# A DeltaNet stage on one core: GpSimd's operations in thirds, its substitution behind VectorE's, transposes and projections in another order

## The reference

```
qkv, z, ab = split(h @ w_in)
q, k, v = silu(centred_conv(qkv))                 # width 4, per channel
q = l2norm(q) * 128**-0.5 ; k = l2norm(k)
g, beta from ab                                   # per token, head and direction
# per chunk of C tokens, gc = cumsum(g):
decay = exp(where(i >= j, gc_i - gc_j, -inf))
a_mat = where(i > j, beta_i * (k @ k.T) * decay, 0) + eye(C)
u, w  = solve(a_mat, [v * beta, k * beta * exp(gc)])      # unit lower triangular
qk = (q @ k.T) * decay ; qg = q * exp(gc) ; kd = k * exp(gc_last - gc)
# scan over the chunks:
v_new = u - w @ S ; o = qg @ S + qk @ v_new ; S = S * exp(gc_last) + kd.T @ v_new
o = rmsnorm(o_f + reverse(o_b)) * silu(z) ; out = o @ w_out
```

## Time and profile before

| what | us |
|---|---|
| median of 3 runs | 3733.95 (3731.53 to 3744.8) |
| the profiled execution's own time | 3739.49 |
| its span, first to last instruction | 3737.7 |
| TensorE busy, of the span | 3344.0 (89%) |
| VectorE, GpSimd, ScalarE busy | 2001.9, 1144.6, 1044.5 |

### The profile page before, as it was taken

One profiled execution on the slowest core, in us unless ns is written; L12 is line 12 of the kernel. 1 busy time (PEld: TensorE's weight loads), 2 busy tenths in 40 slices (PEclk: granted clock), 3 DMA queues, 4 the chain that ended last, 5 costly groups with the idle time before them and its releaser, 6 DMA issues. The chain is left out here.

```text
span 3737.7 us, 51893 instructions
## 1 busy us (share of the span) xinstructions
PE 3344.0 (89%) x20310; PEld 3185.9 (85%) x20310; DVE 2001.9 (54%) x2743; ACT 1044.5 (28%) x1619; POOL 1144.6 (31%) x797
## 2 busy tenths in 40 slices
PE   4985699899999999779999989989898999999996
PEld 2982489799999999678888878878787999999995
DVE  8757653653444335856776776776746222232217
ACT  3226440311111111243534534434423111111110
POOL 2213101321212112245654654654533121121211
PEclk7997799999999999889999999999999999999998
DMA  4520101121211121131231231231320111111111
GB/s 166 185 101 8 59 1 43 71 79 63 90 63 68 63 85 63 68 84 39 67 67 40 66 80 26 67 80 26 99 86 29 46 41 46 41 46 40 41 46 68
DMA packets 103577, 237.92 MB, mean 64 GB/s; under 512 B 8108, under 2 KB 61132, under 8 KB 100428
## 3 DMA queue, kind: packets, MB, share of 16 engines
q1 hardware_dynamic: 103372, 234.82, 20.0%
HBM read 217.54 MB, written 17.26 MB: 63 GB/s over the span
## 5 line engine op out<-in xcount | busy, mean ns | idle before, releaser
L55 PE MATMUL psum<-h_high,panel_high 128*128 128x384 f32 x3624 | 1249.7, 345 | 99.8 <-DVE h_low L495 76.7
L56 PE MATMUL psum<-h_low,panel_high 128*128 128x384 f32 x3624 | 1226.5, 338 | 0.0
L57 PE MATMUL psum<-h_high,panel_low 128*128 128x384 f32 x3624 | 1225.8, 338 | 0.0
L187 POOL TENSOR_TENSOR panel_low<-panel_raw,panel_high 128x1024 fp32r<-128x1024 f32 x196 | 486.3, 2481 | 1715.2 <-ACT panel_high L182 1670.4
L55 PEld LDWEIGHTS psum<-h_high,panel_high 128*128 128x128 f32 x3624 | 691.7, 191 | 145.6 <-issue 94.1
L56 PEld LDWEIGHTS psum<-h_low,panel_high 128*128 128x128 f32 x3624 | 693.0, 191 | 0.0
L57 PEld LDWEIGHTS psum<-h_high,panel_low 128*128 128x128 f32 x3624 | 691.7, 191 | 0.0
L847 DVE TENSOR_TENSOR ffn_product<-ffn_silu_gate,psum 128x1152 f32<-128x1152 f32 x44 | 59.6, 1354 | 709.9 <-PE psum L57 708.5
L182 ACT ACTIVATE panel_high<-panel_raw 128x1024 fp32r<-128x1024 f32 x195 | 205.1, 1052 | 628.5 <-PE psum L57 561.1
L55 PE MATMUL psum<-ffn_mid_high,panel_high 128*128 128x384 f32 x1056 | 355.3, 336 | 12.2 <-DVE x L650 7.5
L57 PE MATMUL psum<-ffn_mid_high,panel_low 128*128 128x384 f32 x1056 | 354.3, 335 | 0.0
(11 more groups left out here) (336 smaller groups left out, 4812.1 us busy)
## 6 DMA issues: line engine op xcount, KB each, us to landing
panel_raw<-in_stream SPq DMA_DIRECT2D x197, 512.0 KB, 3.3
ffn_mod_panels<-in_wmod SPq DMA_DIRECT2D x24, 1024.0 KB, 7.6
dn_rep<-blocks_spill SPq DMA_DIRECT2D x16, 1152.0 KB, 7.8
in_mod_panels<-in_wmod SPq DMA_DIRECT2D x16, 1024.0 KB, 5.5
dn_qg<-rows_spill SPq DMA_DIRECT2D x16, 576.0 KB, 15.9
first_mod_panels<-in_wmod SPq DMA_DIRECT2D x8, 1024.0 KB, 14.0
x<-in_x SPq DMA_DIRECT2D x3, 1536.0 KB, 14.3
x<-in_x SPq DMA_DIRECT2D x1, 4608.0 KB, 15.5
```

Of the source, the lines that this page charges most:

```text
L55: pe.matmul(out, wh, xh, start=first, stop=False)
L56: pe.matmul(out, wh, xl, start=False, stop=False)
L57: return pe.matmul(out, wl, xh, start=False, stop=last)
L187: pool.tensor_tensor(self.wl[buf][:], self.raw[buf][:], self.wh[buf][:].bitcast(F32), ALU.subtract).then_inc(self.split_low.sem, 1)
```

## The change

- GpSimd: the whole-width operations (subtracting sums and adding masks in `exponents`, the diagonal masks, both `decayed_q`, both `kd`, `gated`) are issued as three of 384 columns, and `split` in the heads as two halves of 512. The semaphore rises with the last piece.
- GpSimd begins `substitute` for direction 1 only when VectorE has ended direction 0 (`sub_step[0]` at 31 in the head).
- VectorE: the second `expand` stands behind the sixth slot (`EXPAND = 5`), and the fifth step of v's convolution behind the fifth slot instead of the sixth.
- The first step of k's convolution for the next head goes from VectorE to ScalarE, behind its copy of k's last tile.
- TensorE: the transposes of k (`nine(1, dn.kn, None, True)`) come right behind the reading of k by k, ahead of `tile(3, 0)`; the spread for the output's norm behind `tile(3, 0)`; the sums for q behind `tile(3, 1)`. ScalarE takes `k_tok` accordingly earlier.
- The two final products of the scan's first step go to banks 0 and 1 instead of 3 and 4, and the wait for ScalarE's copies of them moves from the scan's first step to the projection group that next writes bank 0.
- SP fetches the next head's first rows when q by k is done, and the second ones when the values are done, as both before.

```diff
@@ SP
                     sp.wait_ge(qg_ready, 2 * h + 2)
+                    sp.wait_ge(grp_full, full_count(h, FULL_QK, True))
+                    rows(h + 1, 0, dn.rows[0]).then_inc(rows_full, 16)
                     sp.wait_ge(u_full, 2 * h + 2)
-                    for d in range(2):
-                        rows(h + 1, d, dn.rows[d]).then_inc(rows_full, 16)
+                    rows(h + 1, 1, dn.rows[1]).then_inc(rows_full, 16)
@@ GpSimd
             def split(h, j):
-                s.pool_split(pool, 4 * h + (p0 + j), (p0 + j) % 2)
+                p, buf = 4 * h + (p0 + j), (p0 + j) % 2
+                pool.wait_ge(s.split_high.sem, p + 1)
+                for half in (slice(0, 512), slice(512, 1024)):
+                    i = pool.tensor_tensor(s.wl[buf][:, half], s.raw[buf][:, half], s.wh[buf][:, half].bitcast(F32),
+                                           ALU.subtract)
+                i.then_inc(s.split_low.sem, 1)
+
+            def thirds(op):
+
+                for n in range(0, NT, 3):
+                    i = op(slice(n, n + 3))
+                return i
...
-                    mul(dn.osum[:], dn.osum[:], dn.silu_z[:]).then_inc(y_done, 1)
+                    o, z = by_block(dn.osum), by_block(dn.silu_z)
+                    thirds(lambda n: mul(o[:, n], o[:, n], z[:, n])).then_inc(y_done, 1)
...
                 if not first:
                     gated(h)
+                pool.wait_ge(sub_step[0], 31 * h + 31)
                 substitute(pool, 1, h)
@@ TensorE
                     if m == (24 if k_reads == 1 else 40):
                         pe.wait_ge(k_read, k_reads)
+                    if m == 24 and k_reads > 1:
+                        pe.wait_ge(fin_ready, 2 * k_reads - 2)
...
                 read(READ_KK)
+                nine(1, dn.kn, None, True).then_inc(grp_full, 1)
+                read(READ_V)
+                tile(3, 0)
+                read(READ_KTR)
                 if not first:
                     pe.wait_ge(post_step, 2 * h - 1)
                     spread(dn.osq).then_inc(post_full, 1)
-                read(READ_V)
-                tile(3, 0)
+                tile(3, 1)
                 pe.wait_ge(sq_ready["q"], h + 1)
                 sums(7, dn.kd[0]).then_inc(l2_full, 1)
-                tile(3, 1)
+                tile(3, 2)
                 if not first:
                     pe.wait_ge(post_step, 2 * h)
-                nine(1, dn.kn, None, True).then_inc(grp_full, 1)
-                tile(3, 2)
                 pe.wait_ge(recip, 2 * h + 2)
-                read(READ_KTR)
                 spread(dn.kd[0]).then_inc(l2_full, 1)
...
-                    mm = pe.matmul(psum[:, 3 + d, 0:P], blk(dn.kd[d], 0), blk(dn.ub[d], 0), start=True, stop=True)
+                    mm = pe.matmul(psum[:, d, 0:P], blk(dn.kd[d], 0), blk(dn.ub[d], 0), start=True, stop=True)
...
-                    if t == 0:
-                        pe.wait_ge(fin_ready, 2 * h + 2)
@@ ScalarE
                         evac_tile(dn.raw["k"], 2, 2).then_inc(k_read, 1)
+                        act.wait_ge(k_read, h + 2)
+                        act.activation(dn.kn[:], dn.raw["k"][:], ACT.Copy, scale=at_head(dn.conv, 1, h + 1, 2)
+                                       ).then_inc(conv_step["k"], 1)
@@ VectorE
-            V_STEPS = {0: (0,), 1: (1,), 2: (2,), 3: (3,), 5: (4,), 6: (5,), 7: (6,)}
+            EXPAND = 5
+            V_STEPS = {0: (0,), 1: (1,), 2: (2,), 3: (3,), 4: (4,), 6: (5,), 7: (6,)}
...
-                        if d == 0 and c == TURN - 2:
+                        if d == 0 and c == EXPAND:
                             dve.wait_ge(y_stored, 16 * h + 16)
                             expand(dve, 1, h)
...
-                k_steps = {2: (0,), 3: (1, 2), 4: (3, 4), 5: (5, 6)}
+                k_steps = {3: (1, 2), 4: (3, 4), 5: (5, 6)}
```

More of the change, by code:

```diff
@@ L1743, in delta_stage @@
     (FULL_KK, FULL_KTR, FULL_K0, FULL_K1, FULL_VTR, FULL_W0, FULL_QK, FULL_W1, FULL_Q0, FULL_Q1) = range(1, 11)
-    (READ_KK, READ_V, READ_L2Q, READ_KTR, READ_Z, READ_K0, READ_K1, READ_VTR, READ_W0, READ_QK, READ_W1
+    (READ_KK, READ_V, READ_KTR, READ_L2Q, READ_Z, READ_K0, READ_K1, READ_VTR, READ_W0, READ_QK, READ_W1
      ) = range(1, 12)
@@ L1930, in exponents @@
                     pool.wait_ge(rows_full, 32 * h + 32)
-                    pool.tensor_tensor(r, r, dn.gc_next[:, d, :].rearrange("p (n o) -> p n o", o=1
-                                                                           ).to_broadcast([P, NT, P]),
-                                       ALU.subtract).then_inc(dec_step, 1)
+                    thirds(lambda n: pool.tensor_tensor(
+                        r[:, n], r[:, n], dn.gc_next[:, d, n].rearrange("p (n o) -> p n o", o=1
+                                                                        ).to_broadcast([P, 3, P]), ALU.subtract)
+                           ).then_inc(dec_step, 1)
                     pool.wait_ge(dec_step, 3 * h + (d + 2))
-                    pool.tensor_tensor(r, r, mask(dn.low[:, d, :], NT), ALU.add).then_inc(dec_ready, 1)
+                    thirds(lambda n: pool.tensor_tensor(r[:, n], r[:, n], mask(dn.low[:, d, :], 3), ALU.add)
+                           ).then_inc(dec_ready, 1)
             split(0, 1)
@@ L1946, in decayed_q @@
                         pool.wait_ge(s_loaded, 64 * h + 64)
-                    mul(dn.qg[d][:], dn.qn[:], dn.qg[d][:]).then_inc(qg_ready, 1)
+                    qg, qn = by_block(dn.qg[d]), by_block(dn.qn)
+                    thirds(lambda n: mul(qg[:, n], qn[:, n], qg[:, n])).then_inc(qg_ready, 1)
                 def kd(d):
@@ L1955, in kd @@
                         pool.wait_ge(kd_ready, 2 * h + 1)
-                    mul(by_block(dn.kd[d]), by_block(dn.k_tok), const(EK_, d)).then_inc(kd_ready, 1)
+                    to, k_tok, decay = by_block(dn.kd[d]), by_block(dn.k_tok), const(EK_, d)
+                    thirds(lambda n: mul(to[:, n], k_tok[:, n], decay[:, n])).then_inc(kd_ready, 1)
                 def decayed():
@@ L1982, in gated @@
                     pool.wait_ge(post_step, 2 * h)
-                    mul(dn.osum[:], dn.osum[:], dn.silu_z[:]).then_inc(y_done, 1)
+                    o, z = by_block(dn.osum), by_block(dn.silu_z)
+                    thirds(lambda n: mul(o[:, n], o[:, n], z[:, n])).then_inc(y_done, 1)
                 for d in range(2):
                     pool.wait_ge(decay_act, 4 * h + (d + 1))
-                    mul(by_block(dn.ub[d]), by_block(dn.pt[d]), mask(dn.diag[:], NT)).then_inc(dec_ready, 1)
+                    to, pt = by_block(dn.ub[d]), by_block(dn.pt[d])
+                    thirds(lambda n: mul(to[:, n], pt[:, n], mask(dn.diag[:], 3))).then_inc(dec_ready, 1)
                 split(h, 3)
@@ L2266, in body @@
                     pe.wait_ge(s.split_low.sem, p0 + 4 * DN_H + 1)
+                    pe.wait_ge(fin_ready, 2 * h + 2)
                     for c in range(LAST):
@@ L2373, in body @@
                 take(dn.raw["v"], 0)
+                full(FULL_KTR)
+                take(dn.k_tok, 1)
                 if not first:
@@ L2381, in body @@
                 root(dn.kd[0], 7, D).then_inc(grp_read, 1)
-                full(FULL_KTR)
-                take(dn.k_tok, 1)
                 used(h, 3)
@@ L2429, in body @@
                 for d in range(2):
-                    act.activation(dn.fin[d], psum[:, 3 + d, 0:P], ACT.Copy).then_inc(fin_ready, 1)
+                    act.activation(dn.fin[d], psum[:, d, 0:P], ACT.Copy).then_inc(fin_ready, 1)
                 for t in range(4):
@@ L2608, in body @@
                         for m in k_steps.get(t, ()):
-                            if m == 0:
-                                dve.wait_ge(k_read, h + 2)
                             conv("k", dn.kn, h + 2, h + 1, m)
```

## The result

| | before | after |
|---|---|---|
| median, us (four runs each) | 3732.74 (3726.13 to 3744.80) | 3675.45 (3666.97 to 3677.24) |
| the profiled execution's own time | 3739.49 | 3666.97 |
| ratio | | 0.9838 (0.9809 to 0.9868) |

The change makes the kernel 57.3 us faster, 1.6%. The forecast was 28.6 us (3705): direction and range were right, the size was half of what came.

What follows compares the result with a forecast made beforehand. TensorE, busy 89% of the span, was taken as the bound: whatever makes it wait is paid. Terms of 2.0 us in eight heads (16) plus 1.8 in seven (12.6) gave 28.6 us, 3705 for the median, range 3668 to 3728.

Steps and rivals of the forecast that it cites:

- The scan: Next head's convolution steps in the scan: thirds and earlier rows leave 3.8 of 5.6 us lost, gain 1.8 in seven heads.
- the scan is freed whole: Rival: exponents are over before the scan's convolution steps begin, 3 us more in seven heads, 3684; chance 0.20.
- Thirds do nothing: Rival: GpSimd's next third goes ahead of waiting VectorE, the scan keeps its loss, only the substitution gains: 3718; chance 0.07.
- The substitution: VectorE's substitution, with GpSimd's held back, shrinks from 14.8 to 11.7 us: gain 3.1 a head.
- TensorE's order: Wait before q's sums covered, but TensorE's wait at the first expansion goes to about 3 us: -0.1 a head.
- The sixth slot and the clock: Second expansion, per head: -0.5 for later masks, -0.7 for the later slot, -0.9 for half clock behind TensorE's longer wait.
- the clock takes it all: Rival: half clock follows both expansion waits in every head, 12 to 28 us more, 3717 to 3733; chance 0.15.
- The banks: Scan's first step: TensorE no longer waits for ScalarE to empty two banks, gain 0.6 a head.
- q's norm: First stretch, VectorE's steps for q and third reciprocal: gain 0.5 a head, bounds -0.5 and 2.
- no wait in front of q's sums: Sign of being right: TensorE's wait of 3.15 us ahead of the sums for q is gone, covered by a projection tile.
- the exponents 7 us behind the scan's start: Sign of being right: GpSimd's exponents start some 9 us after the scan's start instead of 14.
- the second substitution as the path: Rival: GpSimd's substitution ends late and VectorE's expansion in the sixth slot waits; 5 us late gives 3753; chance 0.10.

Runs made afterwards that it cites:

- experiments 1 to 3: Kernel after with GpSimd's operations whole again, 3697.5 us; with both row transfers late as before, 3673.4; with both edits, 3717.6.
- experiment 1: Kernel after with GpSimd's operations whole again instead of in pieces, early rows kept: 3697.5 us, ratio 0.9916.
- Experiments 7 and 8: Kernel after with TensorE's order of before: 3695.8 us; kernel before with only GpSimd's wait for VectorE's substitution added: 3722.2 us.
- experiment 4: Kernel after without GpSimd's wait for the end of VectorE's substitution, second expansion still behind the sixth slot: 3722.8 us, ratio 0.9978.
- experiment 5: Kernel after with the second expansion back behind the fifth slot and v's fifth step behind the sixth, GpSimd's wait kept: 3653.7 us, ratio 0.9802.
- Experiment 6: Kernel after without GpSimd's wait and with the second expansion back behind the fifth slot: 3685.9 us, ratio 0.9875.
- experiments 5 and 10: Kernel after with the second expansion back behind the fifth slot, 3653.7 us; kernel after with k's first convolution step back on VectorE, 3663.9 us.

## Why the prediction was right in direction and half in size

**The scan: the step that failed.** The term was 1.8 in seven heads and measured 4.7, which is 20 of the 44 us by which the profiled executions exceed the sum. The record went: the pairs lose 5.6 today, "I take 3.8 left". Left were 2.3. The record let each of the two operations of a pair wait for a whole third (1.8 us a pair, 2.4 with the split) and took nearly all of that. A third takes 0.8 (2.40 for three), and the excess of a pair over 1.54 was 0.86, 1.40 (part of it beside the split's halves) and 0; with late rows, where thirds lie over all of the last two pairs, 1.01 and 0.77. That is about one third a pair, not one an operation. With whole operations it was up to 3.4. The early rows had been counted as a share of the same sum; experiments 1 to 3 show two ways to one gain. With early rows, whole operations lie beside steps without convolution, and there the new values, which read PSUM, stayed at 0.61 us (below); only the first pair is then caught. Nor had the loss any spare time to disappear in: from the fourth step to the seventh the recurrence went from 17.3 to 13.2 us, 4.1, more than the 3.3 that the pairs gained. The last 0.5 lies at the scan's end: four of the six heads before had half clock in the scan and none after, and in two of the four, the fourth and the sixth, the part from the seventh new values on was 1.6 us longer than in the other heads.

So the rival that "the scan is freed whole" came nearer in time (3684) with a wrong reason: the exponents were not over before the steps began, and need not be. "Thirds do nothing" is refuted by experiments 1 to 3.

**The substitution: right mechanism, mis-sized.** New length 10.6 for 11.7, gain 4.6 for 3.1. The split had 0.7 in the sum and cost 0.77 - 0.29 = 0.5; the gated product had 2.9 and cost 3 x 0.7 = 2.1 (0.98, 0.97 and 0.98 for operations of 0.28 or 0.29 us). The product is no shorter than the record had it: its thirds take 3.09 us. But in the 1.0 us of each third VectorE also does one operation of its own, 0.3 us with the step to the next; the record put the whole product on top of operations that it had counted already. Whole operations (experiment 1) gave 11.5, so cutting brought 0.9 here: in the fourth head of that kernel the first two operations take 1.38 us behind the split and 2.65 behind the product, a loss of 1.1 and 2.4 for 0.5 and 2.1. Two thirds of it are thus the split's, and the product in thirds costs nearly what it costs whole, as the record said. By the Trainium skill (SBUF — State Buffer, "Who interferes with whom") the shared port pair is an exclusive lock, held for a whole instruction. The rows agree that VectorE waits until the piece in front of it has ended (0.5 us for the split, 0.7 for each of three thirds), and no lengthened operation of it in this stretch exceeds 0.98; what does not follow is that cutting frees nothing: with late rows it took 3.7 us a head off the scan (32.2 to 28.5).

**TensorE's order: -0.1, measured 0.6 and, undone, 20 us.** The wait at the first expansion was to grow to 3 us. It stayed at 1.37, because in the fourth head VectorE's expansion came 4.5 us earlier and TensorE 4.6 (its wait began 46.2 us from the head's norm before, and begins at 41.5 now). The 0.6 of the table is half clock, not the order's own. That the order is worth nothing was wrong as a way of counting: it was set against VectorE's gain, and the gain was booked whole under the substitution. Experiments 7 and 8 show that without the order only part of VectorE's gain arrives.

**The sixth slot and the clock: right sign, another form.** -2.1 in all, measured -1.3. The expansion starts 17.3 us after the first, as before (18 forecast), and GpSimd is done 0.8 us ahead (0 to 2 forecast). The wait is 2.50 us, not 3.3, and without a half clock the stage takes 19.9 us, as before. What it costs came in two of the six heads from the second to the seventh, at 5.5 us each: 1.5 behind the first expansion and 4.0 behind the second (1.8 a head over the six). The record held waits of 1.26 and 1.61 us as too short for a half clock; a wait of 1.37 was followed by one in two heads. The trace of before had such a case already, in its third head:

```profile
1963.15 0.87 PE L2137 MATMUL psum<-ident,dn_tt 128*128 128x128 f32 x6 [1.76 <-DVE dn_tt L1831]
```

```profile
1965.10:1968.50 3.40, 3.40 (x19) 3.40 (x18) 0.00 (x0) 1.30 (x3) 2.63 (x6) 0.50 0.42 167
```

The rival in which the clock takes it all did not come in this kernel; its picture, half clock behind both expansions in every head, came in the one of experiment 4, which also lacks GpSimd's wait.

**The rest.** The banks 0.6 and measured 0.9; q's norm 0.5 and 0.3; no wait in front of q's sums; the exponents 7 us behind the scan's start for 9 forecast. The rival on the other side, the second substitution as the path, did not come: GpSimd ended where the record put it, 16.5 us behind VectorE for "about 17", and the price of ending late would have been small, since 0.46 us of waiting for it in experiment 5 went with a faster kernel.

**In sum.** Beyond the terms forecast, the profiles gained 2.9 in the scan (seven heads), 1.5 in the substitution, 0.7 at the first expansion and 0.8 in the slots (eight heads each): 20 + 12 + 5 + 6 = 43, with the 28.6 about the 72.5 measured. By the medians it is 57; the profiled execution of after is 8.5 us below its median, about as much as one or two more heads with a half clock (5.5 each) would add. Which heads had one in the runs without a profile cannot be seen. Experiment 6 says by medians where the shortfall lies: the wait and the sixth slot together were to bring 8 us (3.1 - 0.5 - 0.7 - 0.9 in eight heads) and bring 10 on top of the rest, the other parts 21 and bring 47 (1.3 a head of it in the substitution, 13.9 us there; the scan is 28.2).

**Not settled.** Why the same wait of 1.37 us at the first expansion is followed by half clock in some heads and not in others, and why the kernels of experiments 5 and 10 have none from the second to the seventh head. These kernels differ from the one after by about what the clock costs it, so their order among each other may hang on it.

## What to carry to other kernels

Where short operations stand behind another engine's long ones, cutting the long ones and moving them beside operations that read PSUM are two ways to one gain: price them as alternatives, and price the cut by the pieces that the operations meet: here about one third for a pair of steps in the scan, and one for each short operation in the substitution, less the operation's own time. Before terms of different engines are added up, ask for each whether the next engine is there in time to take it; a gain of VectorE may come through only in part (1.7 of 3.6 us here) where TensorE's order stays as it was. And a place in the order that costs nothing in undisturbed heads can still cost by the clock: look at which heads carry half-clock stretches before a difference of half a per cent is put down to the work itself.

## What the runs showed of the hardware that was not expected

- Whole operations of GpSimd on SBUF of 2.1 to 2.4 us did not lengthen operations of VectorE that read PSUM: the new values took 0.61 us beside them as without. The convolution steps, SBUF to SBUF, went from 1.54 to 3.88 us a pair (experiment 1). The lines below are VectorE's and GpSimd's in that kernel, fourth head.

```profile
2149.00 0.61 DVE L2604 SCALAR_TENSOR_TENSOR dn_vf<-psum,dn_head_consts,dn_ub 128x128 f32<-128x128 f32 x2 [1.23 <-PE psum L2245]
```

```profile
2147.44 2.38 POOL L1940 TENSOR_TENSOR dn_qn<-dn_qn,dn_neg_masks 128x1152 f32<-128x1152 f32 x1
2149.78 2.11 POOL L1936 TENSOR_TENSOR dn_v_tok<-dn_v_tok,dn_next_sums 128x1152 f32<-128x1152 f32 x1
2151.97 2.39 POOL L1940 TENSOR_TENSOR dn_v_tok<-dn_v_tok,dn_neg_masks 128x1152 f32<-128x1152 f32 x1
```

- In the profiled execution of the kernel after, a wait of TensorE of 1.37 to 1.39 us was followed by 3.4 us at the 1.2 GHz level in two of the heads from the second to the seventh and by none in four; in those two the next wait was 3.69 us and was followed by 6.8 us at that level, in the four 2.50 and followed by none.
